# Slot table laid out by rank, loaded by SyncE, with the round count read ahead of the first gathering

## What is computed

```python
h = h + concat([o_a, o_b], -1) @ w_out            # projection, residual
xn = rmsnorm(h, norm_ffn_g)                       # (512, 1024)
grp = top_1(softmax(xn @ w_grp + b_grp))          # one of 4 groups
e1, e2 = top_2(softmax(logits_of_group))          # 2 experts in the group
combine[t, e] = g_val * e_val / sum(e_val)        # 0 for experts not chosen
for e in range(N_EXPERTS):
    a = silu(xn @ w_gate[e]) * (xn @ w_up[e])
    y = y + combine[:, e:e+1] * (a @ w_down[e])
h = h + y
out = rmsnorm(h, final_norm_g)
```

## Time and profile before

| | us |
|---|---|
| median of 3 runs | 1636.87 |
| lowest, highest of them | 1632.72, 1638.95 |
| the profiled execution, its own time | 1629.7 |
| its span | 1628.0 |
| PE busy (share of the span) | 1416.1 (87%) |
| DVE, ACT, POOL busy | 439.6, 358.5, 172.1 |
| mean granted TensorE clock | 0.934 |
| expert part of block 1, first gathering to last down product | 517 to 784 |
| expert part of block 2, the same | 1277 to 1604 |

### The profile page before, as it was taken

How to read it: one execution, slowest core, us unless ns; L and a number is a source line. 1 busy time by engine, 2 the same in 40 slices (tenths; PEclk the granted TensorE clock), 3 DMA queues, 4 the chain that set the end, 5 groups by cost and what they waited for, 6 DMA issues and landing times. The chain is left out here.

```text
span 1628.0 us, 23375 instructions
## 1 busy us (share of the span) xinstructions
PE 1416.1 (87%) x10234; PEld 739.8 (45%) x10234; DVE 439.6 (27%) x818; ACT 358.5 (22%) x613; POOL 172.1 (11%) x243
## 2 busy tenths in 40 slices
PE   5989989887897799999599999477889779999995
PEld 3434444577556345544344443466545533333332
DVE  2233315433224011111711000692522300000015
ACT  2023016444222011111411100322532101111112
POOL 5000002254001000000000000240000111000000
PEclk8989999999997799999799999785999789999998
DMA  5351100200245599999612210000241568999983
GB/s 195 112 203 52 52 0 0 105 4 4 58 180 195 210 384 417 418 417 408 265 52 78 78 52 0 1 1 30 75 174 74 182 250 336 358 360 373 345 348 127
DMA packets 77229, 283.82 MB, mean 174 GB/s; under 512 B 17889, under 2 KB 19240, under 8 KB 64834
## 3 DMA queue, kind: packets, MB, share of 16 engines
q1 hardware_dynamic: 65888, 267.40, 42.8%
q0 software_dynamic: 5440, 10.58, 1.9%
q10 hardware_dynamic: 5794, 4.27, 0.8%
HBM read 259.38 MB, written 29.84 MB: 178 GB/s over the span
## 5 line engine op out<-in xcount | busy, mean ns | idle before, releaser
L347 PE MATMUL banks<-mixT,ring 128*128 128x512 f32 x672 | 294.9, 602 | 0.8 <-DVE mixT L2446 0.8
L347 PEld LDWEIGHTS banks<-mixT,ring 128*128 128x128 f32 x672 | 129.9, 194 | 165.5 <-issue 164.2
L2170 PE MATMUL banks<-arena_moe,mixT 128*32 128x512 f32 x768 | 169.5, 594 | 0.0
L2170 PE MATMUL banks<-ring,mixT 128*32 128x512 f32 x768 | 113.0, 598 | 13.0 <-DMA arena_moe<-in_w_up 9.3
L1450 PE MATMUL banks<-ring,mixT 128*128 128x512 f32 x256 | 115.8, 608 | 8.2 <-PEq L51 8.2
L1724 PE MATMUL banks<-G_moe,x_hi_moe 128*128 128x256 f32 (+1 forms) x320 | 83.2, 298 | 0.2 <-DVE G_moe L1770 0.2
L344 PE MATMUL banks<-ring,mixT 128*128 128x512 f32 x192 | 82.9, 593 | 0.0
L1724 PE MATMUL banks<-G_moe,x_lo_moe 128*128 128x256 f32 (+1 forms) x320 | 81.5, 293 | 0.0
L1749 DVE TENSOR_TENSOR mixT<-banks,params 128x512 f32<-128x512 f32 (+1 forms) x64 | 39.9, 624 | 151.3 <-PE banks L1724 99.7
L1450 PEld LDWEIGHTS banks<-ring,mixT 128*128 128x128 f32 x256 | 48.9, 196 | 65.4 <-issue 65.4
L2170 PEld LDWEIGHTS banks<-ring,mixT 128*32 128x32 f32 x768 | 39.1, 111 | 83.5 <-issue 78.4
(11 more groups left out here) (424 smaller groups left out, 1963.5 us busy)
## 6 DMA issues: line engine op xcount, KB each, us to landing
ring<-in_w_in SPq DMA_DIRECT2D x18, 1024.0 KB, 8.0
arena_moe<-in_exp_w_gate SPq DMA_DIRECT2D x16, 1024.0 KB, 13.8
arena_moe<-in_exp_w_up SPq DMA_DIRECT2D x16, 1024.0 KB, 17.1
arena_moe<-in_exp_w_down SPq DMA_DIRECT2D x16, 1024.0 KB, 15.2
ring<-in_exp_w_gate SPq DMA_DIRECT2D x16, 1024.0 KB, 12.1
ring<-in_exp_w_up SPq DMA_DIRECT2D x16, 1024.0 KB, 15.0
ring<-in_exp_w_down SPq DMA_DIRECT2D x16, 1024.0 KB, 17.8
arena_moe<-in_w_gate SPq DMA_DIRECT2D x8, 2048.0 KB, 10.9
```

Source lines behind the costliest of these rows:

```text
L347: last = pe.matmul(bank[:], w[:, c, i * P:(i + 1) * P], m.mixT[:, c, :], start=(c == 0), stop=(c == DC - 1))
L2170: last = pe.matmul(hb[u][T * i:T * (i + 1), :], z.xe[:, j, at:at + T], both[:, :, j, half * 256:half * 256 + 256], start=(j == 0), stop=(j ...
```

## The change

Five edits, all in the expert part.

1. **Layout.** The table lies by rank: entry (rank, expert) instead of (expert, rank). A partition's row is now one piece of 32 or 16 entries (256 or 128 bytes), and the views `raw` and `weight` pick the even or odd experts out of it. Odd experts are read by starting one entry later, so those pieces have 31 or 15 entries. Block 1 needs 2 DMAs with 64 pieces each, block 2 needs 4 with 96, 32, 64 and 64.
2. **Who loads it.** SP in place of ACT: in block 1 between the gate and up loads of body 1's slots 0, 1 and those of slots 2, 3; in block 2 ahead of all loads of body 1. Before it SP now waits for `tabled`, and before `load_gain` for `entries`.
3. **Rounds first.** DVE counts the rounds before the first one-hot matrices, and PE and DVE jump over their `If` before the first gathering instead of behind it. The code in the `If` no longer gathers again.
4. **Positions.** `first_entry` (two small DVE instructions) goes; two fused ones replace the addition.
5. **Stored outputs.** In block 1 `z.outs[0]` is ring slot 1 in place of slot 2, so the loads wait for the first unit of the last body; projection item 1, which goes to the same slot, waits until the 8 additions are done.

```diff
@@ class Slots
-        self.raw, at = m.view(at, bodies, 2, 2, dt=I32)
+        self.rows, at = m.view(at, copies, experts, 2, dt=I32)
+        parity = self.rows.rearrange("p c (e b) v -> p c e b v", b=2)[:, :, :, 0, :]
+        if copies == 1:
+            self.raw = parity.rearrange("p a (i c) v -> p (a i) c v", c=2)
+        else:
+            self.raw = parity.rearrange("p c i v -> p i c v")
@@ class Moe
-        spent = m.ring01[:, 0, 0:NT * D] if self.wide else self.ring23[:, 0, 0:NT * D]
+        spent = m.ring01[:, 0 if self.wide else 1, 0:NT * D]
@@ def load_slots
-        t = self.d.table.rearrange("(i e n) v -> e i n v", e=self.EB, n=self.d.entries)
+        table = self.d.table.rearrange("(n e) v -> n e v", e=self.E)
-        def part(partition, c, e, rank, n):
-            src = t[e][:, bass.ds(first_rank + rank, n), :].rearrange("i n v -> n i v")
-            engine.dma_start(slots.raw[partition:partition + n, :, c, :], src).then_inc(sem, 16)
+        def part(partition, copy, odd, rank, n):
+            src = table[bass.ds(first_rank + rank, n), odd:, :]
+            engine.dma_start(slots.rows[partition:partition + n, copy, 0:self.E - odd, :], src).then_inc(sem, 16)
...
-            for e in range(4):
-                part(64 * (e % 2), e // 2, e, 0, 64)
+            part(0, 0, 0, 0, 64)
+            part(64, 0, 1, 0, 64)
@@ def entries
-        dve.tensor_tensor(z.position, z.rank, z.first_entry, ALU.add).then_inc(ph.sem("entries"), 1)
+        for k in range(2):
+            dve.scalar_tensor_tensor(z.position[:, k, :], z.rank[:, k, :], float(E), one[7 + k], ALU.mult, ALU.subtract).then_inc(ph.sem("entries"), 1)
@@ def load_outputs
-    sp.wait_ge(ph.sem("hidden"), z.units * (z.bodies - 1) + 2)
+    sp.wait_ge(ph.sem("hidden"), z.units * (z.bodies - 1) + (2 if z.wide else 1))
@@ narrow sync
+        sp.wait_ge(out.sem("entries"), ENTRIES)
         load_gain()
         for i in range(1, NB):
             for s in range(4):
+                if i == 1 and s == 2:
+                    sp.wait_ge(out.sem("tabled"), TABLED)
+                    z.load_slots(sp, z.main, 0, ph.sem("slots"))
@@ narrow tensor (vector and the wide program alike)
+        further_pe(pe, further, z, x, x_ring, extra_body)
         first_rows_pe(pe, ph, out, z, gath, yb[0:2])
-        further_pe(pe, further, z, ph, x, x_ring, gath, yb[0:2], extra_body)
@@ narrow vector, last body
-        early(0)
-        early(1)
-        for c in range(2):
-            for n in range(2):
-                y_low_dve(dve, ph, z, 2 * c + n, yb[2 * c + n], z.main.weight[:, NB - 1, c:c + 1])
-        early(2)
+        for t in range(3):
+            early(t)
+        for n in range(2):
+            y_low_dve(dve, ph, z, n, yb[n], z.main.weight[:, NB - 1, 0:1])
         early(3)
+        for n in range(2):
+            y_low_dve(dve, ph, z, 2 + n, yb[2 + n], z.main.weight[:, NB - 1, 1:2])
@@ narrow scalar (the wide one alike)
-            hiddens(ph, i, None if i else load_slots)
+            hiddens(ph, i)
@@ between_programs
-        p_sync(sp, keep)
+        p_sync(sp, lambda: sp.wait_ge(experts.sem("added"), 2 * NT), keep)
@@ expert_block, DVE
             out_vector(dve)
+            rounds(dve)
             onehot_dve(dve, ph, m, z, 0)
             entries(dve)
-            rounds(dve)
```

More of the change, by code:

```diff
@@ L1297, in __init__ @@
         self.units = 3 if self.wide else 2
+        self.loads = 64 if self.wide else 32
         self.most = -(-S // slots)
@@ L1602, in vector @@
         dve.tensor_tensor(one[4], one[2], one[1], ALU.subtract).then_inc(ph.sem("second_less"), 1)
-        for k in range(2):
-            v.mark(dve.tensor_scalar(z.first_entry[:, k, :], one[7 + k], -float(z.d.entries), float(E * z.d.entries - 1), ALU.mult, ALU.add))
         split(NT - 1)
@@ L1652 @@
 TABLED = 16 * 2 * NT
+ENTRIES = 3
 class Further:
@@ L2028, in scalar @@
             else:
-                act.wait_ge(ph.sem("slots"), SLOTS_LOADED)
+                act.wait_ge(ph.sem("slots"), z.loads)
             for c in range(2):
@@ L2072, in first_rows_pe, with further_pe @@
     gather_pe(pe, ph, z, second, 1, None)
-def further_pe(pe, further, z, ph, x, x_ring, first, second, body):
+def further_pe(pe, further, z, x, x_ring, body):
     def end(n):
@@ L2079, in end @@
         pe.wait_ge(x.sem("body_done"), done + 1)
-        gather_pe(pe, x, z, first, 0, None)
-        gather_pe(pe, x, z, second, 1, None)
         for s in range(z.EB):
@@ L2084, in end, with further_dve @@
             pe.wait_ge(x_ring[len(x_ring) // 2 + s], 16 * done + 16)
-        pe.wait_ge(x.sem("gathered_taken"), 4 * done + 4)
+        pe.sem_inc(x.sem("reloaded"), 1)
     further.run(pe, lambda r: None, body, end)
-def further_dve(dve, further, m, z, x, first, second, gain, rest):
+def further_dve(dve, further, z, x, rest):
     def begin(r):
-        dve.wait_ge(x.sem("slots"), SLOTS_LOADED * r + SLOTS_LOADED)
+        dve.wait_ge(x.sem("slots"), z.loads * r + z.loads)
         slots_known(dve, z, z.extra, x.sem("known"), KNOWN * r)
@@ L2102, in body @@
         rest(g, i)
-    def end(n):
-        for half in range(2):
-            turned_rows_dve(dve, x, m, z, second if half else first, gain, n * z.bodies, half)
-    further.run(dve, begin, body, end)
+    further.run(dve, begin, body, lambda n: dve.nop())
 def wide_programs(m, io, z, ph, x, out, gain, ring_sems):
@@ L2554, in project2_programs, with sync @@
     lbc = COLUMN["hg_lb_logits_2"]
-    def sync(sp, keep):
+    def sync(sp, second_free, keep):
         for n in range(6):
+            if n == 1:
+                second_free()
             if n == 2:
```

36 lines of the change are left out of this document (13 added, 23 removed).

## The result

The changed kernel takes 1617.17 us in the median of 7 runs (1616.08 to 1620.04), the kernel before 1632.72 us in 7 runs beside them (1627.53 to 1638.95). The ratio is 0.9907 (95% interval 0.9886 to 0.9928): 15.6 us faster, where 23.8 us had been forecast. The time lies in the forecast range, 4 us above its point of 1613. That flatters the saving: the forecast counted from three runs of the kernel before at 1636.87 us, and the seven beside these lie 4.15 us lower. From their median the same sum gives 1608.9, 8.3 us too low. In the profiled executions the span falls from 1628.0 to 1615.4 us, 12.6 us.

The account below looks back on a forecast made before the run. The prediction took TensorE as the bound, busy 1416.1 of 1628.0 us, with savings only in its pauses or half-clock time. Terms -10.9 - 12.1 + 2.5 - 2.5 - 0.8 = -23.8 us gave 1613 us from 1636.9, range 1605 to 1625.

Parts of the forecast that it names:

- A: Block 2: TensorE's stall before body 0's down products goes, -10.9 us, range -6 to -11.
- B: Block 1: TensorE's stall before body 0's down products goes and these products shorten, -12.1 us.
- C: Block 1: the weight stream, with full DMA engines, takes back part of the gain, +2.5 us, range +0.7 to +5.
- D: End of block 1: stored outputs loaded earlier bring the first total earlier, -2.5 us, range 0 to -4.
- E: Both blocks, rounds read before the gathering: later start, but unbroken gate products; -0.8 us, bounds -6 and +9.5.
- cheap jump: Rival, both blocks: TensorE jumps over the rounds as fast as ScalarE, -29.0 us in all, 1608 us; chance 0.09.
- lost clock: Slower rival, both blocks: TensorE stays at 1.2 GHz through body 0's gate products, +9.4 us, 1646 us; chance 0.04.
- Streams take back more: Rival: block 1's weight stream costs +5 us and a late up load in block 2 costs 3; 1619 us, chance 0.16.
- TensorE pays for the rounds: Rival, both blocks: gathering at half clock and slow gate products, +9.5 us for the rounds; 1623 us, chance 0.13.
- late table: Rival, block 1: the table lands late and ACT stands until 566 instead of 556.5; 1622 us, chance 0.05.

## Why the prediction was right, and where it was not

*A and B, the stalls: right in mechanism and size.* -11.0 for -10.9, -12.2 for -12.1. Body 1's weights were there (no wait at its start), and every edit in which the stall was gone had 25.6 and 15.4 us in these stretches (the kernel before with the rows held back, where it was not, had 35.9 and 26.0). That it took SyncE and long pieces was not needed: either would have served in most places.

*C, the stream of block 1: right.* With the old handling of the outputs, body 1 to first total grew from 216.65 to 219.45, +2.8 for +2.5 (a second profile with the stall in it has 218.0, which would make it +1.4; both lie in the range given). TensorE's waits for `in_exp_w_up` went from 6.2 to 8.6 us. They did not begin a body earlier, as the working had it: the first is in body 4 in both, 0.58 us before and 2.19 after.

*D, the stored outputs: wrong sign.* The forecast was -2.5, the runs show +1.8. Two steps failed. "The loads next in the queue, so the first pair lands near 775.5 to 776", 1.5 to 2 us after the last gate products, where 3.90 was measured (5.51 before): eight loads issued early still come in behind the down weights, and counted from body 1 the first addition starts where it does without the edit (206.8 and 206.9 us). And the working added up VectorE's work, where the first total in fact waited 1.40 us for TensorE's sums, held up by low parts that the new order puts last.

*E, rounds ahead: the step that failed is "I take the same price at the new place".* The price of the jump is a fetch, and has neither the same size nor is it always due. In block 1 no pause beyond the matrices stands before the gathering, as the rival of the cheap jump had it: the skipped code had become short. But where the forecast had no pause behind the gathering, six of eight profiles still have 1.9 to 3.5 us more than VectorE's move needs; what makes it there is open, and the forecast's "none behind the 64 gathering matmuls" failed in block 1. In block 2 the price rose from 3.1 us behind the gathering (the 3.7 us less VectorE's move, 0.65) to 6.2 beyond the matrices, since it now meets full DMA queues where it had met empty ones. At the old place, in the kernel before:

```profile
1286.00:1291.00 5.00, 1.68 (x15) 1.50 (x14) 2.16 (x5) 0.00 (x0) 2.91 (x3) 0.97 0.05 4
```

The share is 0.05 there, and 0.84 at the new place. Five kernels with the rounds ahead in block 2 take 32.0 to 32.3 us from the end of the routing products to the end of the gate products, six with them behind 29.3 to 31.3: +1.7 us, for a forecast of nothing. That the gate products then run unbroken in 13.9 us was right in block 2, and in block 1 in four of eight profiles. The argument against a lost clock, that half clock ended within 6 us of the next work, did not hold in the kernel before itself: in block 2 the clock is still 0.50 at 1283.8, 6.7 us after the gathering's start.

*Not in the forecast at all: bodies 1 to 7 of block 2.* Four kernels with the rounds ahead there, and the rows not held back, took 264.7 to 267.4 us, four with them behind 260.6 to 262.4. In the first, two or three bodies wait 2.3 to 3.5 us for weights, and where a half-clock stretch of 3.41 us follows it adds 1.7 us. The rows carry most of it, as the two runs that held them back with the rounds ahead show (261.2 and 261.1). What tips those bodies is open. An instruction packet of the smaller kind (q14) lies in the window of the long waits of bodies 2 and 5, and these two stay the longest (2.20 and 1.99) without the rows; but other bodies with such a packet wait 1.3 to 2.2 us. The kernel without TensorE's body of the further rounds in block 2 takes 263.6: bodies 2 and 5 wait only 1.29 and 1.72 us there, and body 6 waits 2.89. No run changed the place of the code and nothing else.

*Rivals.* "Streams take back more" came closest to the time for partly wrong reasons: block 1's stream did not, block 2's did, by rows. "TensorE pays for the rounds" was right in kind for block 2, small in size. The rule that block 1's jump becomes cheap and block 2's does not was right for the pause before the gathering in both, where I had given the cheap jump 0.09. The late table and the lost clock did not occur.

The sum by steps of one pair of profiles: -11.0 - 12.2 + 4.2 (C and D) + 0.1 (E in this pair) + 6.9 (bodies 1 to 7 of block 2) - 0.5 (the rest) = -12.5, against -12.6 measured. It closes because the stretches cover the span; the shares in it move by 1 to 3 us from one profile to the next. That the time lies in the range owes something to luck: D was wrong by 4.3 us and block 2's bodies cost 6.9 us for which there was no term, and the range had room for both only because other rivals had widened it.

## What to carry over

A stall that an issuing engine shows in the profile can be costed and taken away with confidence: its length and its cover came out within 0.1 us. Before moving a jump, count what it skips, and look at what the DMA queues carry at the new place, for the code comes over them too. Where weights land only just in time, rows that nobody waits for yet should be made to wait for them: it cost nothing where they were early and gave 3.5 to 6 us of the stretch where they were late.

## What the hardware showed

- Fetching the code behind a jump cost TensorE 3.1 us with nearly empty DMA queues (share 0.09) and 5.2 to 6.2 us with full ones (0.84 in the changed kernel); nothing before the gathering where little or no code was skipped.
- 2048 pieces of 8 bytes held ScalarE for 18.69 us (DMA share 0.96) and SyncE for 8.09 (0.97) or 3.25 us (0.19); 256 long pieces held SyncE for 2.02 and ScalarE for 2.23 us.
- 0.30 MB of rows between issue and landing of 2 MB weights went with a landing 2 us later, and a wait of that length was often, not always, followed by 3.41 us at clock 0.50: one of 2.36 us was, one of 2.80 us was not (the expectation for the held rows has it behind each wait of 2.8 us or more; the 2.80 us are in the kernel with the outputs put back).
